# Two-block transformer kernel: the last expert's outputs are added to turned sums of the first fifteen in PSUM, and the plain sum is completed amid the next block's query-key product

## The reference, cut to what matters

```
x = first_block(x, ...)        # ends: x = x + sum over 16 experts of
                               #   gate * scatter( (silu(xe @ w_gate) * (xe @ w_up)) @ w_down )
h = x                          # second_block
hn = rms_norm(h, norm1_g)      # h * rsqrt(mean(h*h)) * g, over all 1024 columns
proj = hn @ w_in               # of which "qk2" below: 1024 -> 1024 columns
```

## Time and profile before

| | |
|---|---|
| median of 3 runs | 1475.92 us (1474.6 to 1476.16) |
| the profiled execution | 1476.04 us, of which the span from first to last instruction 1474.3 |
| busy in the span | PE 77%, PEld 47%, DVE 32%, ACT 25%, POOL 3% |
| read from memory | 491.52 MB, 334 GB/s over the span |
| the chain that ended last | DMA 54%, PE 40%, DVE 4%, ACT 1%, issue 1% |

### The profile page before, as it was taken

One profiled execution on the slowest core, in us unless ns is written; L12 is line 12 of the kernel. 1 busy time (PEld: TensorE's weight loads), 2 busy tenths in 40 slices (PEclk: granted clock), 3 DMA queues, 4 the chain that ended last, 5 costly groups with the idle time before them and its releaser, 6 DMA issues.

```text
span 1474.3 us, 20259 instructions
## 1 busy us (share of the span) xinstructions
PE 1132.6 (77%) x8449; PEld 687.0 (47%) x8449; DVE 469.8 (32%) x891; ACT 374.9 (25%) x623; POOL 41.1 (3%) x92
## 2 busy tenths in 40 slices
PE   9999999975666556756656566565665999999998
PEld 8887887521212212213112122121121678999887
DVE  6988885100000000000000000000000578675546
ACT  6658663100001001001001000000100475465434
POOL 1220120000000000000000000000000000000000
PEclk9999999988778878688788778888887999999999
DMA  8663529999999999999999999999999754555551
GB/s 306 201 250 109 198 87 380 392 426 426 427 427 430 428 427 427 428 430 427 426 429 427 429 428 427 430 427 427 428 429 429 293 185 172 172 183 190 193 186 50
DMA packets 58777, 493.33 MB, mean 335 GB/s; under 512 B 6698, under 2 KB 8292, under 8 KB 34148
## 3 DMA queue, kind: packets, MB, share of 16 engines
q1 hardware_dynamic: 58580, 492.07, 82.2%
q10 hardware_dynamic: 144, 0.52, 0.1%
HBM read 491.52 MB, written 1.05 MB: 334 GB/s over the span
## 4 chain that ended last, share of the span: by engine, by line
DMA 54%; PE 40%; DVE 4%; ACT 1%; issue 1%; SPq 0%; DVEq 0%; ACTq 0%
DMA arena<-in_expert_w_down 18%; DMA arena<-in_expert_w_up 18%; DMA arena<-in_expert_w_gate 17%; PE ps L1918 13%; PE ps L2011 7%; PE ps L1923 6%; PE ps L2365 4%; PE ps L2387 2%; DVE w_split L1188 1%; PE ps L1990 1%; PE ps L2181 1%; PE ps L2212 1%; PE ps L2125 1%; PE ps L2100 1%; PE ps L1994 0%
## 5 line engine op out<-in xcount | busy, mean ns | idle before, releaser
L2365 PE MATMUL ps<-arena 128*32 128x512 f32 x1024 | 169.3, 799 | 111.2 <-DMA arena<-in_expert_w_up 58.1
L2365 PE MATMUL ps<-ring,arena 128*32 128x512 f32 x1024 | 159.5, 755 | 120.4 <-DMA ring<-in_expert_w_up 64.6
L1188 DVE TENSOR_TENSOR w_split<-ring,w_split 128x1024 fp32r<-128x1024 f32 (+3 forms) x178 | 201.5, 1139 | 94.2 <-ACT w_split L754 93.1
L754 ACT ACTIVATE w_split<-ring 128x1024 fp32r<-128x1024 f32 (+3 forms) x178 | 175.4, 991 | 182.9 <-PE ps L1923 128.4
L1640 DVE TENSOR_TENSOR arena<-arena,ps 128x512 f32<-128x512 f32 x16 | 11.0, 687 | 555.9 <-PE ps L2365 555.9
L2365 PEld LDWEIGHTS ps<-arena 128*32 128x32 f32 x1024 | 33.1, 130 | 238.6 <-DMA arena<-in_expert_w_up 97.5
L2365 PEld LDWEIGHTS ps<-ring,arena 128*32 128x32 f32 x1024 | 32.0, 123 | 239.1 <-DMA ring<-in_expert_w_up 102.6
L2011 PE MATMUL ps<-hT_hi,w_split 128*128 128x256 f32 x608 | 111.8, 285 | 0.1
L2387 PE MATMUL ps<-arena 128*32 128x256 f32 x1072 | 81.4, 454 | 34.9 <-DMA arena<-in_expert_w_down 31.4
L2387 PE MATMUL ps<-ring,arena 128*32 128x256 f32 x896 | 71.8, 476 | 39.8 <-DMA ring<-in_expert_w_down 36.8
L1630 DVE COPY arena<-ps 128x128 f32<-128x128 f32 x32 | 9.3, 291 | 273.3 <-PE ps L2346 273.3
(11 more groups left out here) (360 smaller groups left out, 1378.8 us busy)
## 6 DMA issues: line engine op xcount, KB each, us to landing
ring<-in_expert_w_up SPq DMA_DIRECT2D x36, 2048.0 KB, 35.9
arena<-in_expert_w_gate SPq DMA_DIRECT2D x36, 2048.0 KB, 35.7
ring<-in_expert_w_gate SPq DMA_DIRECT2D x28, 2048.0 KB, 36.6
arena<-in_expert_w_up SPq DMA_DIRECT2D x28, 2048.0 KB, 37.2
arena<-in_expert_w_down SPq DMA_DIRECT2D x25, 2048.0 KB, 36.2
ring<-in_expert_w_down SPq DMA_DIRECT2D x21, 2048.0 KB, 37.1
ring<-in_w_ff SPq DMA_DIRECT2D x32, 1024.0 KB, 5.1
ring<-in_w_in SPq DMA_DIRECT2D x23, 1024.0 KB, 5.0
```

Of the source, the lines that this page charges most:

```text
L754: act.activation(w_split[:, n % WBUFS, 0, 0:cols], slot_view(slot, cols)[:, n % 2, :], ACT.Copy).then_inc(split_hi, 1)
L1188: dve.tensor_tensor(buf[:, 1, :], w, buf[:, 0, :].bitcast(F32), ALU.subtract).then_inc(split_lo, 1)
L2365: m = pe.matmul(ps[j * CAP:(j + 1) * CAP, bank, :], xe[:, kt, :], w[r][:, j * FCOL:(j + 1) * FCOL], start=kt == 0, stop=kt == KT - 1, skip ...
```

## The change

Only the handing over from the last expert to the second block is changed.

- Sum of fifteen: while expert 15 is still at work (its inputs gathered), VectorE copies parts 0 and 2 and ScalarE parts 1 and 3 of banks 4 to 7 to `xs`. `xs` then holds x and fifteen experts.
- Turned sums: after the first down chunk of expert 15 TensorE transposes parts 0 to 2 of it into banks 0 to 2 (`turned_sum`, four transposes each), as the start of an accumulation.
- Turned scatter: the last expert's output isn't scattered to banks 4 to 7. It is added to the turned sums: `turned_scatter(j, k)` multiplies columns k of part j of `ye` (as stationary operand) by part j of `scat`. Parts 0 to 2 come first, then `turned_sum(3)` into bank 3 (which had held `ye` and `scat`), then the two of part 3. `high_stage` reads banks 0 to 3 as before.
- Plain sum: after "qk2" tile 3, and after all `hT_lo` are made, TensorE scatters the last expert's output into banks 0 to 3 (`scatter(0, True)`, 8 matmuls), VectorE adds the four banks to `xs` (counted by `x_summed`), and only then come squares, root and diagonals.
- VectorE's list becomes: low 0; `low_stage` 0 to 3; low 1; `low_stage` 4 to 7; low 2 and 3; four adds; low 4; squares; root; diagonals; low 5 to 7. ScalarE's square waits for the four adds, with high 2 to 5 ahead of it.
- Experts 14 and 15 are taken out of the loops and written straight; `keep_clock` ahead of the third and fourth down chunk is left in expert 15 alone (now into bank 4), and the `WARM_MIX` = 2 matmuls after it go to bank 4.

```diff
@@ -720,8 +720,7 @@
             def segment_starts(buf):
                 return buf.rearrange("p (m b c) -> p m b c", m=2, b=3)[:, :, 0:2, 0:1]
 
-            pool.wait_ge(sum_dve, 2)
-            pool.wait_ge(sum_act, 2)
+            pool.wait_ge(x_summed, 4)
             step(pool.memset(whole_stick, 0.0))
             whole = whole_stick.rearrange("p (m c) -> p m c", m=2)
             for first in (whole[:, :, 0:P], whole[:, :, P:2 * P + 1]):
@@ -970,36 +969,40 @@
                                    scale=rstd_x[:, h:h + 1])
             e.then_inc(rexp_done, 1)
 
+            def expert(e, final=False):
+
+                act.wait_ge(scat_done, e + 2)
+                act.wait_ge(e_scatter, e + 1)
+                act.activation(scat, ps[:, 3, 256:512], ACT.Copy).then_inc(scat_ready, 1)
+                if final:
+                    act.wait_ge(gather_done, IN_ROWS * EXPERTS)
+                    for j in (1, 3):
+                        act.activation(part_of_x(j), summed(j), ACT.Copy).then_inc(sum_act, 1)
+                act.wait_ge(chunk_used, EXPERT_CHUNKS * e + T1_RELEASES + IN_CHUNKS)
+                act.wait_ge(hid_ready, e + 1)
+                act.activation(hid_g, ps[:, 0, :], ACT.Silu).then_inc(silu_done, 1)
+                act.wait_ge(hidT_done, e + 2)
+                act.activation(hidT, ps[:, 2, :].rearrange("p (c t) -> p c t", c=4), ACT.Copy).then_inc(hidT_ready, 1)
+                act.wait_ge(chunk_used, EXPERT_CHUNKS * e + T1_RELEASES + EXPERT_CHUNKS)
+                act.activation(ye, ps[:, 3, 0:DCOL], ACT.Copy).then_inc(ye_ready, 1)
+
             act.sem_inc(ye_ready, 1)
-            with act.Fori(0, EXPERTS // PAIR) as pair_i:
+            with act.Fori(0, EXPERTS // PAIR - 1) as pair_i:
                 for j_e in range(PAIR):
-                    e = pair_i * PAIR + j_e
-                    act.wait_ge(scat_done, e + 2)
-                    act.wait_ge(e_scatter, e + 1)
-                    act.activation(scat, ps[:, 3, 256:512], ACT.Copy).then_inc(scat_ready, 1)
-                    act.wait_ge(chunk_used, EXPERT_CHUNKS * e + T1_RELEASES + IN_CHUNKS)
-                    act.wait_ge(hid_ready, e + 1)
-                    act.activation(hid_g, ps[:, 0, :], ACT.Silu).then_inc(silu_done, 1)
-                    act.wait_ge(hidT_done, e + 2)
-                    act.activation(hidT, ps[:, 2, :].rearrange("p (c t) -> p c t", c=4), ACT.Copy).then_inc(hidT_ready, 1)
-                    act.wait_ge(chunk_used, EXPERT_CHUNKS * e + T1_RELEASES + EXPERT_CHUNKS)
-                    act.activation(ye, ps[:, 3, 0:DCOL], ACT.Copy).then_inc(ye_ready, 1)
+                    expert(pair_i * PAIR + j_e)
+            for e in range(EXPERTS - PAIR, EXPERTS):
+                expert(e, e == EXPERTS - 1)
 
 
             act.wait_ge(chunk_used, ALL_EXPERTS)
             high_parts("qk2", 0, 1)
-            act.wait_ge(bank_scattered, 3 * EXPERTS - 1)
-            act.activation(part_of_x(1), summed(1), ACT.Copy).then_inc(sum_act, 1)
-            act.wait_ge(e_scatter, EXPERTS + 1)
-            act.activation(part_of_x(3), summed(3), ACT.Copy).then_inc(sum_act, 1)
             high_stage("mix", 0, "norm1_g_2", range(0, 2))
             high_parts("qk2", 1, 2)
             high_stage("mix", 0, "norm1_g_2", range(2, KT))
-            high_parts("qk2", 2, 3)
-            act.wait_ge(sum_dve, 2)
-            act.wait_ge(sum_act, 2)
+            high_parts("qk2", 2, 6)
+            act.wait_ge(x_summed, 4)
             square_half()
-            high_parts("qk2", 3)
+            high_parts("qk2", 6)
             high_parts("v2", 0, 3)
             act.wait_ge(rstd_ready, 3)
             act.wait_ge(tile_used, done("qk2"))
@@ -1612,7 +1615,7 @@
 
             dve.sem_inc(hid_ready, 1)
             dve.wait_ge(ffn_vec_ready, 1)
-            def expert(e):
+            def expert(e, final=False):
 
                 for h in range(HALVES):
                     dve.tensor_scalar(onehot[:, h, :], slot_ids[:, :], slot_t[:, h, bass.ds(e, 1)], rstd_x[:, h:h + 1],
@@ -1634,6 +1637,10 @@
                     dve.tensor_tensor(xe.rearrange("p (c r) s -> p c r s", r=IN_ROWS)[:, :, r, :],
                                       ps[:, r, P:2 * P].rearrange("p (c s) -> p c s", s=CAP),
                                       w, ALU.mult).then_inc(xe_ready, 1)
+                if final:
+                    dve.wait_ge(e_scatter, EXPERTS)
+                    for j in (0, 2):
+                        dve.tensor_copy(part_of_x(j), summed(j)).then_inc(sum_dve, 1)
                 dve.wait_ge(silu_done, e + 1)
                 dve.wait_ge(chunk_used, EXPERT_CHUNKS * e + T1_RELEASES + 2 * IN_CHUNKS)
                 dve.wait_ge(hidT_done, e + 1)
@@ -1641,25 +1648,26 @@
 
             for e in range(PAIR):
                 expert(e)
-            with dve.Fori(1, EXPERTS // PAIR) as pair_i:
+            with dve.Fori(1, EXPERTS // PAIR - 1) as pair_i:
                 for j_e in range(PAIR):
                     expert(pair_i * PAIR + j_e)
-
-
-            for j in (0, 2):
-                dve.wait_ge(bank_scattered, 3 * EXPERTS - 2 + j)
-                dve.tensor_copy(part_of_x(j), summed(j)).then_inc(sum_dve, 1)
+            for e in range(EXPERTS - PAIR, EXPERTS):
+                expert(e, e == EXPERTS - 1)
+
+
             low_parts("qk2", 0, 1)
             low_stage("mix", 0, "norm1_g_2", range(0, 4))
             low_parts("qk2", 1, 2)
             low_stage("mix", 0, "norm1_g_2", range(4, KT))
-            low_parts("qk2", 2, 3)
-            dve.wait_ge(sum_dve, 2)
-            dve.wait_ge(sum_act, 2)
+            low_parts("qk2", 2, 4)
+            for j in range(4):
+                dve.wait_ge(bank_scattered, 3 * (EXPERTS - 1) + j + 1) if j < 3 else dve.wait_ge(e_scatter, EXPERTS + 1)
+                x = part_of_x(j)
+                dve.tensor_tensor(x, ps[:, j, :].rearrange("p (h d) -> p h d", h=HALVES), x, ALU.add).then_inc(x_summed, 1)
+            low_parts("qk2", 4, 5)
+            dve.wait_ge(x_summed, 4)
             square_half()
-            low_parts("qk2", 3, 4)
             norm(2, squared=True)
-            low_parts("qk2", 4, 5)
 
             for h in range(HALVES):
                 dve.tensor_scalar(diag[:, h * P:(h + 1) * P], ident[:, :], rstd_x[:, h:h + 1], None, ALU.mult).then_inc(diag_ready, 1)
@@ -2335,7 +2343,32 @@
 
                 return slot if isinstance(slot, list) else [slot[:, r * WIDE // n:(r + 1) * WIDE // n] for r in range(n)]
 
-            def expert(e, last, weights, first=False):
+            def turned_sum(j):
+
+                m = 0
+                for k in range(2):
+                    for h in range(HALVES):
+                        kt = 2 * j + k
+                        m = pe.matmul(ps[:, j, k * T + h * P:k * T + (h + 1) * P], xs[:, h, kt * P:(kt + 1) * P], ident[:, :],
+                                      start=k == 0 and h == 0, stop=False, skip_group_check=True)
+                return m
+
+            def turned_scatter(j, k):
+
+                return pe.matmul(ps[:, j, k * T:(k + 1) * T], ye[j * CAP:(j + 1) * CAP, k * P:(k + 1) * P],
+                                 scat[j * CAP:(j + 1) * CAP, 0:T], start=False, stop=True, skip_group_check=True)
+
+            def scatter(bank, fresh):
+
+                for j in range(4):
+                    for h in range(HALVES):
+                        m = pe.matmul(ps[:, bank + j, h * DCOL:(h + 1) * DCOL], scat[j * CAP:(j + 1) * CAP, h * P:(h + 1) * P],
+                                      ye[j * CAP:(j + 1) * CAP, :], start=fresh and h == 0, stop=True, skip_group_check=True)
+                    if j < 3:
+                        m.then_inc(bank_scattered, 1)
+                m.then_inc(e_scatter, 1)
+
+            def expert(e, last, weights, first=False, final=False):
 
                 pe.wait_ge(onehot_ready, 2 * e + 2)
                 pe.wait_ge(hid_ready, e + 1)
@@ -2377,8 +2410,13 @@
                 pe.wait_ge(scat_ready, e + 1)
                 pe.wait_ge(hidT_ready, e + 1)
                 for c in range(OUT_CHUNKS):
+                    if final and c == 1:
+                        pe.wait_ge(sum_dve, 2)
+                        pe.wait_ge(sum_act, 2)
+                        for j in range(3):
+                            turned_sum(j)
                     if last and c >= OUT_CHUNKS - 2:
-                        keep_clock(0, WARM_LAST)
+                        keep_clock(4 if final else 0, WARM_LAST)
                     w = rows_of(weights(2 * IN_CHUNKS + c), OUT_ROWS)
                     for r in range(OUT_ROWS):
                         if c == OUT_CHUNKS - 1 and r == OUT_ROWS - 1:
@@ -2389,13 +2427,17 @@
                                           stop=c == OUT_CHUNKS - 1 and r == OUT_ROWS - 1, skip_group_check=True)
                     m.then_inc(chunk_used, 1)
                 pe.wait_ge(ye_ready, e + 2)
-                for j in range(4):
-                    for h in range(HALVES):
```

(58 more changed lines are left out.)

## The result

The changed kernel takes 1483.27 us (median of 5 runs, 1483.09 to 1484.01), the kernel before 1475.33 (median of 5). The ratio is 1.0054, with a 95% interval of 1.0043 to 1.0065: slower by 7.9 us, about half a percent. The profiled execution took 1483.27 us with a span of 1481.4. 1481.0 had been forecast, with a range of 1478.3 to 1485.0.

The account below looks back on a forecast made before the run. TensorE's rate was taken to bound the query-key product, the weight stream the experts. A 0.6 us handover gain and 5.66 us of delay made +5.1 on the profiled 1476.04 us: 1481.0 after 0.1 for the median, range 1478.3 to 1485.0.

Parts of the forecast that it names:

- rival B: In both scatters, the parts don't run abreast: +8.9 us, 1484.8; chance 0.05.
- the prediction's own signs of being wrong: Low 5 not waiting for the root, two TensorE holes missing, a clock fall there, or the expert stage's end moving.
- a move of the stage's end: Sign of being wrong: the expert stage no longer ends at 1154.3 as before.
- Experts unrolled, keep_clock dropped: nothing: In the expert stage, straight code and fewer keep_clock matmuls cost nothing, covered by the weight stream.
- Rival D: In the expert stage, fewer keep_clock matmuls release weight slots sooner: up to 13.9 us faster, 1467; chance 0.09.
- Twelve transposes in the last expert: nothing: After expert 15's first down chunk, twelve transposes take 1.5 to 2.9 us but cost 0, bound 0.5.
- The handover gains 0.6: Between last scatter and query-key product: TensorE's steps sum to 3.1 us, so the product starts 0.6 us earlier.
- four transposes of part 3: 0.5: In the handover on TensorE, after the turned scatter of parts 0 to 2: four transposes take 0.5 us.
- Sum from S to low 5, 5.66: From tile 3's end (S), VectorE's list makes low 5 ready at S + 10.19 instead of S + 4.53: 5.66 us delay.
- Nothing gives it back: After the query-key product, no later wait absorbs the delay.
- Rival C: Handover gain of 1.9 us and the second block absorb most of the delay: +2.6 us, 1478.5; chance 0.13.
- Rival A, the clock: In the product, TensorE's clock falls in the holes: 1.7 us per half-rate stretch, 1482.7 or 1484.4; chance 0.2.

Follow-up runs that it names:

- straight_only: The kernel before with only experts 14 and 15 written straight and the keep_clock matmuls left in expert 15 alone; 1475.88 us, ratio 1.0001.
- one_hole: The changed kernel with low 5 and 6 moved ahead of the squares, behind the adds; 1479.46 us, ratio 1.0027.
- hole_in_before: The kernel before with 4.4 us of idle multiplications on VectorE ahead of low 5; 1479.65 us, ratio 1.0028.

## Why the prediction was right

The direction and the main mechanism held: VectorE's list behind the plain scatter, two holes in TensorE. The sum was 2.8 us short. The measured +7.9 lies outside the forecast's own bounds, +3.8 to +6.2. It lies in the stated range only because that reached up to rival B, which did not happen; so much of the hit is luck. And one of the prediction's own signs of being wrong came: the granted clock fell there, to 0.50 in the row of that stretch. Another, a move of the stage's end, did not: the last output is copied at 1153.5 instead of 1154.3, within the spread up to A. Step by step:

- *Experts unrolled, keep_clock dropped: nothing.* Right; straight_only shows it alone. Rival D (faster by releases, up to 13.9 us) is out.
- *Twelve transposes in the last expert: nothing.* Right in effect, wrong in the count. They are matmuls on the identity, with two records each, not transposes with one: 24 records, 2.94 us in the changed profile at full clock. They lay beside the stream all the same: the next chunk but one waits for DMA again. TensorE's timeline of the changed kernel:

```profile
1140.79 2.94 PE L2352 MATMUL ps<-ident,xs 128*128 128x128 f32 x24
1143.67 1.93 PE L2425 MATMUL ps<-arena 128*32 128x256 f32 x32
...
1147.82 1.93 PE L2425 MATMUL ps<-arena 128*32 128x256 f32 x32 [1.13 <-DMA arena<-in_expert_w_down]
```

- *The handover gains 0.6.* Wrong, it gains nothing (3.68 against 3.63 us). The step that failed is the second of its list, "four transposes of part 3: 0.5", by the same miscount: eight records, 1.09. The other three held: turned scatter 1.07 (forecast 1.10), part 3's scatter 1.05 (1.0), keep_clock 0.47 (0.5).
- *Sum from S to low 5, 5.66.* It was 6.24 (1.31 + 1.97 + 2.96). The adds took 2.48 for 2.44, and TensorE's holes were 1.62 for 1.91 and 2.65 for 2.65. Low 5's pass came 10.54 behind the scatter's start instead of 10.19: the squares took 1.47 to the next instruction for 1.26, with GpSimd beside them, the root 2.48 for 2.37. The other 0.2 lie at the edges, 0.1 where the scatter begins and 0.1 in the pass behind the last hole. I had moved GpSimd's fills in the sum by their start alone, without asking what they would run beside.
- *Nothing gives it back.* Right: C to D is 294.02 in both kernels. Rival C is out.
- *Rival A, the clock.* It came true beside the forecast, at 1.63 us where 1.7 had been priced; with a chance of 0.2 I had set it too low. The rows showed a fall after 2.97 us of idleness and none after 1.26; two holes of 1.9 and 2.65 lay nearer to the first. One row is thin evidence, though: the same trace has 48 such waits, and behind 3 the clock stayed up. Had I taken it into the forecast, the sum would have been 1482.7.
- *Rival B.* Out: three parts do run abreast, 12 records in 1.07.

In numbers: +5.1 forecast; +0.65 for the handover, +0.6 for the tail, +1.6 for the clock give 7.9.

## What to carry to other kernels

When work is moved into a stretch that one engine bounds, write out the list of the engine that feeds it, from the moved work on, and compare its sum with what the bounding engine still has to do: here 9 us of VectorE's list stood ahead of a 1.2 us step that was due in 4.5, and placing that step earlier took back 6.6 of 7.9 us. Count instructions by their records in the trace, not by the name of the helper. And price holes in TensorE of 2 us and more with the clock as well: where it fell behind one, that cost 1.6 us on top. Whether it falls is a matter of how often; count it over all the like waits of the trace instead of reading one row.

## What was not expected of the hardware

- A hole in TensorE cost 0.3 us more than the idle time that the profile shows (1.97 for 1.63 in one_hole; 3.1 for 2.75 in hole_in_before).
- GpSimd's affine selects and VectorE's float32 operations on SBUF lengthen each other where they overlap: squares 1.43 instead of 1.22 us, two affine selects 1.82 and 2.05 instead of 1.03 in the trace of before, where VectorE's operations out of PSUM and only 0.2 us of a low part ran beside them. GpSimd's first memset (0.74 us) did nothing of the kind: a low part beside it kept its 1.22.
- A hole of 2.75 us left the clock up in two profiles of two. The clock fell in the one profile of a 4.02 us hole, and behind 1.62 and 2.65, and 1.62 and 2.33, with 3 us of work between the two. In the expert stages 568 of 648 waits of 2.9 us or more had it fall. Filling 2 of the 2.65 us with matmuls whose result nobody reads was worth 1.6 us.
